# A mixture-of-experts stage in units of 32 rows, with four-lane products and gate weights copied to a fixed buffer

## The reference, cut to what matters

```python
def hier_moe(h, w_rg, w_re, w_gate, w_up, w_down):
    xf = h.reshape(b * t, dm)                      # 320 rows in all, dm = 2048
    ...                                            # router: one of 4 groups, 2 of its 4 experts
    comb = jnp.sum(jax.nn.one_hot(eid, N_EXPERTS) * wts[..., None], axis=1)
    act = jax.nn.silu(jnp.einsum('nd,edf->nef', xf, w_gate)) * jnp.einsum('nd,edf->nef', xf, w_up)
    act = act * comb[..., None]
    return jnp.einsum('nef,efd->nd', act, w_down)  # added to x, then a last rmsnorm
```

## Time and profile before

| | us |
|---|---|
| median of three runs | 1599.32 |
| lowest, highest | 1598.54, 1600.5 |
| the profiled execution, its own time | 1600.59 |
| its span (first to last instruction) | 1598.7 |
| PE busy | 1470.7 |
| VectorE busy | 608.2 |
| ScalarE busy | 316.0 |
| mean granted TensorE clock, share of full | 0.956 |

### The profile page before, as it was taken

The page is one execution under the profiler, slowest core; times in us unless marked ns, Lnnn a source line. Parts: engine busy times, 40 slices in busy tenths (PEclk is TensorE's granted clock), DMA queues, the critical chain, the costliest instruction groups (busy, mean ns, idle before and its releaser), DMA issues. The chain is left out here.

```text
span 1598.7 us, 21805 instructions
## 1 busy us (share of the span) xinstructions
PE 1470.7 (92%) x8104; PEld 848.5 (53%) x8105; DVE 608.2 (38%) x1162; ACT 316.0 (20%) x702; POOL 43.7 (3%) x55
## 2 busy tenths in 40 slices
PE   7999999998999798778999999769999999999994
PEld 4478887777888566544444565523333333333331
DVE  3154333432654365466100303523343333433335
ACT  3001011222333144366000203101001010010102
POOL 0000000003000000000000000000000000000000
PEclk9999999999999699798999999879999999999998
DMA  9254537434530377202844024979987999969981
GB/s 348 105 172 160 198 134 261 148 134 149 195 113 7 119 238 236 67 1 89 297 152 164 1 106 155 410 261 419 421 360 274 421 421 422 410 251 421 421 311 66
DMA packets 108867, 361.20 MB, mean 226 GB/s; under 512 B 16600, under 2 KB 44288, under 8 KB 80482
## 3 DMA queue, kind: packets, MB, share of 16 engines
q1 hardware_dynamic: 104546, 329.63, 54.5%
q0 software_dynamic: 3744, 22.43, 3.8%
q10 hardware_dynamic: 512, 8.26, 1.4%
HBM read 388.83 MB, written 17.05 MB: 254 GB/s over the span
## 5 line engine op out<-in xcount | busy, mean ns | idle before, releaser
L2499 PE MATMUL bank<-ring,hT_e 128*64 x576 | 267.1, 603 | 1.8 <-DVE hT_e L2574 1.8
L2500 PE MATMUL bank<-ring,hT_e 128*64 128x512 f32 x576 | 267.1, 603 | 0.0
L2595 DVE TENSOR_TENSOR x<-x,bank 128x1024 f32<-128x1024 f32 (+1 forms) x108 | 131.5, 1220 | 213.2 <-PE bank L2487 210.1
L2499 PEld LDWEIGHTS bank<-ring,hT_e 128*64 128x64 f32 x576 | 73.8, 137 | 179.5 <-issue 179.4
L2517 PE MATMUL bank<-W,const 128*64 128x512 f32 x576 | 127.6, 595 | 11.6 <-ACT const L2552 11.6
L1855 PE MATMUL bank<-W,mixT 128*128 128x512 f32 x256 | 113.4, 604 | 1.6 <-DVE mixT L2090 1.6
L2487 PE MATMUL bank<-const,own_rows 64*128 64x512 f32 (+1 forms) x408 | 95.3, 632 | 0.0
L2517 PEld LDWEIGHTS bank<-W,const 128*64 128x64 f32 x576 | 41.1, 137 | 84.6 <-issue 84.1
L1855 PEld LDWEIGHTS bank<-W,mixT 128*128 128x128 f32 x256 | 49.1, 193 | 63.5 <-issue 61.4
L2500 PEld LDWEIGHTS bank<-ring,hT_e 128*64 128x64 f32 x576 | 73.7, 137 | 0.0
L2550 ACT ACTIVATE gate<-bank 64x512 f32<-64x512 f32 x18 | 10.6, 588 | 307.6 <-PE bank L2500 307.6
(11 more groups left out here) (425 smaller groups left out, 2029.5 us busy)
## 6 DMA issues: line engine op xcount, KB each, us to landing
ring<-in_w_exp_gate SPq DMA_DIRECT2D x80, 1024.0 KB
ring<-in_w_exp_up SPq DMA_DIRECT2D x72, 1024.0 KB
W<-in_w_exp_down SPq DMA_DIRECT2D x72, 1024.0 KB
raw<-in_w_in SPq DMA_DIRECT2D x10, 2048.0 KB
raw<-in_w_in SPq DMA_DIRECT2D x8, 2096.0 KB
W<-in_w_out SPq DMA_DIRECT2D x3, 4096.0 KB, 13.6
k_in<-in_cache_sel_k SPq DMA_DIRECT2D x64, 128.0 KB
v_in<-in_cache_sel_v SPq DMA_DIRECT2D x64, 128.0 KB, 3.3
```

What stands on the lines that cost most here:

```text
L2499: pe.matmul(GATE[0:NS, :], hT[:, c, :], w_g[:, c, :], start=(c == 0), stop=(c == KC - 1))
L2500: mm = pe.matmul(GATE[UP, :], hT[:, c, :], w_u[:, c, :], start=(c == 0), stop=(c == KC - 1))
L2595: ins = dve.tensor_tensor(x[0:rows, r, cols], x[0:rows, r, cols], src, ALU.add)
```

## The change

Turns become units of 32 rows. With 32 rows, the array is used in four lanes: `gate_up` makes, per chunk, four products of 256 columns (the two halves of gate and of up), `down` four of 512 columns into one bank, and `move` is three groups of four products, with 32 rows each of `own_rows` as weights, into four banks. A row is gathered in quarters, and all layouts follow (4 rows of the weights to a partition in each quarter). The adds are the same six of 1024 columns per unit. `y` is copied by ScalarE alone.

PE reads gate weights from a fixed buffer `w_g`. ScalarE copies them there from one of two alternating ones (`gate_slot`), a quarter at a time, in every unit (`copy_gate`). Loads are issued in the order up, down, gate; the gate is one expert ahead (`ahead` without the + 1, wait for `g_loaded` at 16 turn + 16), and gate 2 isn't loaded ahead of the stage.

```diff
-TURNS_MAX = NE + 2 * (SEQ + NS) // NS
+UNIT = 32
+UNITS_EACH = TOK // UNIT
+TURNS_MAX = NE + 2 * TOK // UNIT
 ...
                     for r in range(TILES):
-                        if r == 2:
-                            sp.wait_ge(made, 24)
-                            for q, load in enumerate(gate_loads(2)):
-                                sp.wait_ge(g_loaded[q], 32)
-                                sp.dma_start(*load).then_inc(g_loaded[q], 16)
 ...
+        w_g = ring[:, 0, :].rearrange("p (c n) -> p c n", n=FF)
         w_d = W[:, 1, :].rearrange("p (c n) -> p c n", n=D)
 ...
-        def gate_unit(e):
-            return (e * 2 + 2) % 3 * 2
+        def gate_slot(e):
+            return e % 2 * 2 + 2
 
         quarter = lambda q: slice(4 * q, 4 * q + 4)
 
         def gate_loads(e):
-            g = A["w_exp_gate"][0, bass.ds(e, 1)].rearrange("o (h p c) f -> (o p) h c f", h=2, p=P)
-            w_g = ring[:, bass.ds(gate_unit(e), 1), :].rearrange("p o (c n) -> p (o c) n", n=FF)
-            return [(w_g[:, quarter(q), :], g[:, q // 2, quarter(q % 2), :]) for q in range(4)]
+            g = A["w_exp_gate"][0, bass.ds(e, 1)].rearrange("o (h p c) f -> (o p) h c f", h=4, p=P)
+            held = ring[:, bass.ds(gate_slot(e), 1), :].rearrange("p o (c n) -> p (o c) n", n=FF)
+            return [(held[:, quarter(q), :], g[:, q]) for q in range(4)]
 ...
+            return [(w_u[:, quarter(q), :], up[:, q]) for q in range(4)]
 
         def down_loads(e):
-            d = A["w_exp_down"][0, bass.ds(e, 1)].rearrange("o (p c) n -> (o p) c n", c=4)
-            return [(w_d[:, q, :], d[:, q, :]) for q in range(4)]
+            d = A["w_exp_down"][0, bass.ds(e, 1)].rearrange("o (h p c) n -> (o p) h c n", h=2, p=P)
+            return [(w_d[:, q, :], d[:, q // 2, q % 2, :]) for q in range(4)]
 ...
-                    dve.tensor_scalar(ahead[:, :], owner_f[:, :], 1.0, float(NE - 1), ALU.add, ALU.min)
+                    dve.tensor_scalar(ahead[:, :], owner_f[:, :], float(NE - 1), None, ALU.min)
 ...
-            MOVE_AFTER = {2: 0, 6: 1, 10: 2, 13: 3, 15: 4}
+            MOVE_AFTER = {3: 0, 10: 1, 15: 2}
 ...
                     def load_gate_ahead(turn):
                         following, before = ahead_of(turn), ahead_of(turn - 1)
                         for q, (dst, src) in enumerate(gate_loads(following)):
-                            sp.wait_ge(g_loaded[q], turn * 16 + 32)
+                            sp.wait_ge(g_loaded[q], turn * 16 + 16)
+                            sp.wait_ge(g_copied[q], turn)
                             sp.dma_start(dst, src, cond=(following > before)).then_inc(g_loaded[q], 16)
 
                     with sp.Fori(1, n) as turn:
                         e, previous = expert_of(turn), expert_of(turn - 1)
                         load_up(turn, e, previous)
+                        load_down(turn, e, previous)
                         load_gate_ahead(turn)
-                        load_down(turn, e, previous)
 ...
                 def _(pe):
                     def turn_rows(turn):
                         pe.wait_ge(gathered, turn * 16 + 16)
+                        for k in range(4):
+                            mm = pe.transpose(ROWS_B[:, k * P:k * P + P], rows_in[:, k:512:4], ident)
+                        mm.then_inc(h_turned, 1)
+
+                    def move(turn, r):
+                        if r == 0:
+                            pe.wait_ge(own_ready, turn + 1)
+                            pe.wait_ge(y_copied, turn + 1)
+                        pe.wait_ge(added, turn * 3 + r + 3)
                         pe.sem_inc(pe_passed, 1)
-                        for k in range(8):
-                            for h, lane in enumerate(LANES):
-                                mm = pe.transpose(ROWS_B[h][:, k * NS:k * NS + NS], rows_in[lane, k:1024:8], ident[lane, lane])
-                        mm.then_inc(h_turned, 1)
-
-                    def move(turn, k):
-                        r, half, to = MOVES[k]
-                        if k == 0:
-                            pe.wait_ge(own_ready, turn + 1)
-                            pe.wait_ge(y_copied_a, turn + 1)
-                            pe.wait_ge(y_copied_d, turn + 1)
-                        pe.wait_ge(added, turn * 5 + k + 4)
-                        pe.sem_inc(pe_passed, 1)
-                        for n in range(4) if half is None else (2 * half, 2 * half + 1):
-                            lane = LANES[n % 2]
-                            rows = slice(0, P) if r < 2 else LANES[n // 2]
-                            mm = pe.matmul(bank2[to][rows, 512 * (n % 2):512 * (n % 2) + 512], own_rows[lane, P * r:min(P * r + P, TOK)],
-                                           y[lane, n // 2, :], start=True, stop=True)
+                        for n, lane in enumerate(LANES):
+                            mm = pe.matmul(bank[n][0:TILE_ROWS[r], :], own_rows[lane, P * r:P * r + TILE_ROWS[r]], y[lane, :], start=True, stop=True)
                         mm.then_inc(moved, 1)
 
-                    def gate_up(turn, e, moving=None):
-                        w_g = ring[:, bass.ds(gate_unit(e), 1), :].rearrange("p o (c n) -> p (o c) n", n=FF)
-                        pe.wait_ge(h_copied, turn * 2 + 2)
+                    def gate_up(turn, moving=None):
+                        pe.wait_ge(h_copied, turn + 1)
                         for q in range(4):
-                            pe.wait_ge(g_loaded[q], turn * 16 + 16)
+                            pe.wait_ge(g_copied[q], turn + 1)
                             pe.wait_ge(u_loaded[q], turn * 16 + 16)
                             pe.sem_inc(pe_passed, 1)
-                            for c in range(4 * q, 4 * q + 4):
-                                pe.matmul(GATE[0:NS, :], hT[:, c, :], w_g[:, c, :], start=(c == 0), stop=(c == KC - 1))
-                                mm = pe.matmul(GATE[UP, :], hT[:, c, :], w_u[:, c, :], start=(c == 0), stop=(c == KC - 1))
-                                if c == 4 * q + 3:
+                            for k in range(4):
+                                c = 4 * q + k
+                                for n, lane in enumerate(LANES):
+                                    cols = slice(256 * (n % 2), 256 * (n % 2) + 256)
+                                    mm = pe.matmul(GATE[lane, 0:256], hT[:, k, q, :], (w_g if n < 2 else w_u)[:, c, cols], start=(c == 0), stop=(c == KC - 1))
+                                if k == 3:
                                     mm.then_inc(gu_used[q], 1)
                                 if moving is not None and c in MOVE_AFTER:
                                     move(moving, MOVE_AFTER[c])
 ...
+                        for c in range(2):
+                            mm = pe.transpose(ACT_T[:, c * 2 * UNIT:(c + 1) * 2 * UNIT], gate[UP, c:256:2], ident[UP, UP])
                         mm.then_inc(a_turned, 1)
                         pe.wait_ge(a_copied, turn + 1)
-                        pe.wait_ge(added, turn * 5 + 4)
                         for q in range(4):
                             pe.wait_ge(d_loaded[q], turn * 16 + 16)
-                            for n in range(4):
-                                mm = pe.matmul(bank[n // 2][LANES[n % 2], :], actT[:, q, :], w_d[:, q, 512 * n:512 * n + 512], start=(q == 0), stop=(q == 3))
+                            for n, lane in enumerate(LANES):
+                                mm = pe.matmul(DOWN[lane, :], actT[:, q % 2, q // 2, :], w_d[:, q, 512 * n:512 * n + 512], start=(q == 0), stop=(q == 3))
                             mm.then_inc(d_used[q], 1)
 ...
-                    def step(turn):
+                    def copy_gate(turn, q):
+                        held = ring[:, bass.ds(gate_slot(expert_of(turn)), 1), :].rearrange("p o (c n) -> p (o c) n", n=FF)
+                        act.wait_ge(g_loaded[q], turn * 16 + 16)
+                        act.copy(w_g[:, quarter(q), :], held[:, quarter(q), :]).then_inc(g_copied[q], 1)
+
+                    def activate(turn):
                         act.wait_ge(gu_used[3], turn + 1)
-                        act.activation(gate[UP, :], GATE[0:NS, :], ACT.Silu).then_inc(silu_ready, 1)
+                        act.activation(gate[UP, :], GATE[0:P // 2, 0:256], ACT.Silu).then_inc(silu_ready, 1)
+
+                    def keep_act(turn):
                         act.wait_ge(a_turned, turn + 1)
-                        act.copy(actT, ACT_T[:, 0:4 * NS].rearrange("p (k r) -> p k r", k=4)).then_inc(a_copied, 1)
+                        act.copy(actT, ACT_T[:, 0:4 * UNIT].rearrange("p (c h r) -> p c h r", c=2, h=2)).then_inc(a_copied, 1)
+
+                    def keep_y(turn):
                         act.wait_ge(d_used[3], turn + 1)
-                        act.copy(y[:, 0, :], bank[0]).then_inc(y_copied_a, 1)
-
-                    with act.Fori(0, count(act, 0)) as turn:
-                        step(turn)
```

(62 more changed lines are left out.)

119 lines of the change are left out of this document (47 added, 72 removed).

## The result

The changed kernel takes **1640.99 us** (median of 4 runs, 1639.07 to 1643.81), the kernel before, run beside it on the same chip, 1599.91 (1598.54 to 1603.33): a ratio of **1.0255, 95% interval 1.0232 to 1.0277**, slower by 2.6%. The forecast was 1604, slower by 0.3%, and its range ended at 1624. The direction is right (it had been given a chance of 0.53), and the size is wrong by 37 us. The profiled execution has a span of 1638.7 us where 1603.2 was forecast, so it is 35.5 us that the text has to find.

What follows compares the result with a forecast made beforehand. PE bound the old kernel, DMA close behind; afterwards waits for loads absorb PE's saving. Load stream 1060 + 182 + 209 + 102 + 20.4, then landing, clock and tail, gave span 1603.2, time 1604 us; range 1585 to 1624.

Steps and rivals of the forecast that it cites:

- A unit on PE: TensorE's time for one 32-row unit: 16.3 us, 26 units making 424 us against 519 before.
- rival C: Moves of four row groups go in pairs, 2.0 us and not 1.25: 1624 us in all; chance 0.12.
- rival E: ScalarE's gate copies take 3 us or more beside the traffic: 1625 us or later; chance 0.03.
- rival D: Loads themselves slower beside ScalarE's copies, 2.6 us each for 2.49: 1618 us; chance 0.10.
- Start: Before the expert stage: earlier gather, one drain, first product at 1054.3; first byte of expert 1's up load at 1060.
- Tail: From the last down product to the end: 23.2 us, against 24.3 before.
- A two-unit expert: From one up load's first byte to the next expert's: 34.8 us, six times, 209 in all.
- Three-unit: Expert of three units, the two-unit sum and one more unit: 51.0 us, twice, 102 in all.
- the 4.5 of clock: Allowance for PE at half clock after idling in experts 3 and 8 and at the end: 4.5 of 8.5 us.
- A: Faster: the queue hides the second unit's wait in multi-unit experts, and no lower clock: 1589 us; chance 0.30.
- B: Nothing changes: wait partly hidden, two-unit experts at 34.2 us, 1600 us in all; chance 0.17.
- A's far end: No ScalarE wait at all in second units: two-unit experts 33.2 us, three-unit 44, 1576 us in all.

Runs made afterwards that it cites:

- e2: Changed kernel, but ScalarE's gate copies in repeated units wait for their own expert's gate, not the next one's: 1603.7 us.
- h1: Changed kernel with ScalarE and SyncE waiting for their own expert's gate in repeated units, small copies first, fewer and earlier register reads: 1571.1 us.
- e4: Changed kernel with SyncE's two gate register reads doubled, between the down and gate loads: 1653.0 us.
- f3: Changed kernel with SyncE's two gate register reads moved ahead of the down loads: 1632.6 us.
- e1: Changed kernel with ScalarE keeping the activations before, not behind, its copy of the next gate's quarter 0: 1631.0 us.
- f1: Changed kernel with ScalarE keeping the activations before gate copy 0, and y before copies 1 and 2: 1609.6 us.
- g1: Kernel before, still with 64-row units and two lanes, given only the new gate path (buffers, ScalarE copies, load order): 1605.2 us.
- e3: Changed kernel with the loads in the old order up, gate, down: 1646.9 us.

## Why the prediction was wrong in size

Point by point, by its own steps:

- **A unit on PE**, 16.3 us: 16.11, and 15.82 where ScalarE reads its registers once a unit. Right. The move of four row groups holds up the stream for 1.07 us (1297.88 to 1298.95) where 1.25 was taken; rival C (pairs, 2.0) falls. By the Trainium skill ("TensorE: Matmul & The Clock Gate", Measured speedup vs the span model) the estimate was 1.1, and the trace agrees.
- **ScalarE's copies**, 1.90: 1.897 over 104. Right; rival E falls. The second unit's wait for gate(e+1), with keep_act and down behind it, was foreseen, and is there. **Loads** at 421 GB/s: right, rival D falls. **One-unit expert** 30.4: 30.5. **Start**: the first up load's bytes begin at some 1057.6, 2.4 us before the 1060 of the forecast (issued 1056.18, the engines at a share of 0.18 from 1056 to 1058). **Tail** 23.2: 24.25 (1614.45 to 1638.7).
- **A two-unit expert, 34.8: on the mean 40.1** (from real up load to real up load; one-unit experts ahead of 3 and 8 taken at 30.5). Three-unit, 51.0: 54.9 and 56.0. Eight experts, 40.5 us more in all; less the 4.5 of clock that stood apart, less 2.4 at the start, and with 1.05 of tail and some 0.5 of one-unit experts it is 35 of the 35.5 us. This is the step that failed, in what it puts behind the landing of the gate: 3.5 for down and 3.3 from there to the next up load's first byte, where 6.18 and 6.9 were measured. In expert 6, term by term:
  - from the first byte of up to the landing of the gate's first quarter: 24.45 (1263.4 to 1287.85), forecast 25.4. The 1.7 us between up and down didn't occur; landing is nearer 2 than 1.2. Both small.
  - copy, keep_act, hand-over: 2.2, forecast 2.6.
  - **down: 6.18, forecast 3.5.** PE had idled 5.7 us and started at the lower clock. The eight downs on the chain take 4.97 to 6.48 us, 46.7 in all where 3.64 each would be 29.1: 17.6 us, where 4.5 had been allowed for the whole stage, for experts 3 and 8 and the very end. The forecast's own terms leave PE idle before down in every such expert; it gave the clock a thought only where the wait was 11 us.
  - **from down's end to the first byte of the next up load: 6.9, forecast 3.3** (first quarter of gate and up 1.9, issue and first byte 1.4). This is the largest single miss, 3.6 us eight times (the eight passes agree within 0.02 us), 29 us. The forecast let the up load go out as soon as PE freed its buffer. But SyncE takes its queue in order, and the repeated unit's empty loads stand ahead: the down group waits for d_used of the unit whose down had just ended, then four reads and four empty gate loads follow. I had counted only the loads that move bytes. The gap of 1.9 us between load groups was in the trace of before too, as 1103.53 (end of the up group) to 1105.42; there nothing waited for it.
- **The rivals.** A was to decide at 34 us a two-unit expert: it was 40, on the other side. B (34.2 a two-unit expert) falls with it. A's far end can be held against e2, which takes ScalarE's wait away: 33.2 us a two-unit expert had been reckoned without it, and experts 5 and 6 take 33.3; but a three-unit one was put at 44 and takes 52.5, and the whole 1603.7 and not 1576. It is 47.5 once SyncE's wait for the landing has gone too (h1). No rival had the mechanism that came, SyncE's pass; the range was built around ScalarE's and PE's terms, and left it out.
- **What would show it**: 26 silus, yes. Experts 5, 6 and 9 alternately 16.3 and 18.5 apart: 16.1 and 22.6 to 23.6. Dips of 3 to 4 us: 7 to 8; the 20 us of a three-unit expert: some 23. PE idle 20% of the stage: 24% from 1060 to 1570.

The registers' share is shown both ways (e4, f3), ScalarE's order by e1 and f1, the wait itself by e2, SyncE's wait for the landing by h1. The share of the clock isn't shown by itself: e1 and f1 bring the down products back to 95 us together with the rest of the wait, and the products of gate and up grow there from 197.8 to 218.8 and 213.6.

## What to carry to other kernels

When a loop treats repeated work with the same instructions as new work, walk each in-order queue through the repeated pass as well: an empty load, its wait and its register reads stand ahead of the next real one. Write a wait's count for the data the step needs, not for the number of passes; the difference was 37 us on ScalarE and 21 to 29.5 on SyncE. And a shorter unit of work doesn't only use an engine better: it makes more repeated passes, and each meets every wait that a long unit had covered.

## What the runs showed of the hardware

- TensorE at 1.2 GHz after a short wait: PE idle for 5.7 us before down, the granted clock 0.50 from 1288.5 to 1295 and 1.00 again from 1295.5, and down at 6.18 us in place of 3.64. In the eight experts of several units it is 4.97 to 6.48, behind 5.6 to 5.9 us of waiting in six of them and 10.6 in experts 3 and 8. The Trainium skill ("TensorE: Matmul & The Clock Gate", Part 1: The HAM clock gate) describes it as a throttle that activity releases; the rows agree. I had expected it of the 11 us waits only. It came behind shorter ones than 5.7 too: 2.02 us in e1 (0.50 from 1296 to 1298.5) and 1.44 us in g1 (0.50 from 1365.5 to 1368.5).
- Loads that are queued together move 422 GB/s (changed kernel, 1280 to 1290); in e3 the same 1 MB loads, sent as PE frees the quarters (four in 7.68 us), 328 to 393.
- A pair of register reads on SyncE costs 1.1 to 1.3 us, an empty conditional load 0.42 (1.68 for four), and there is 0.65 us more between two groups. A repeated unit's pass from down's end to the issue of the next real load is 5.9 us with no byte of weights moved.
